# The MLP's up projection by Strassen's identity, seven half products for eight per pair of units, with token sums made once

## The reference

```python
def finish_layer(x, o_a, o_b, ga, gb, p_emb, w_oa, w_ob, w_o, g_ffn, w_up, w_down, g_ple, w_ple_gate, w_ple):
    ya = o_a.reshape(n, t, A_WIDTH).astype(x.dtype) @ w_oa
    yb = o_b.reshape(n, t, B_HEADS * B_V_DIM).astype(x.dtype) @ w_ob
    x = x + (jax.nn.sigmoid(ga) * ya + jax.nn.sigmoid(gb) * yb) @ w_o
    x = x + jnp.square(jax.nn.relu(rms_norm(x, g_ffn) @ w_up)) @ w_down
    x = x + jax.nn.sigmoid(rms_norm(x, g_ple) @ w_ple_gate) * (p_emb @ w_ple)
    return x
```

## Time and profile before

| What | Value |
|---|---|
| median of 3 runs | 1930.64 us (1929.19 to 1931.61) |
| span of the profiled execution | 1926.3 us |
| PE busy | 1867.4 us, 97% |
| PEld busy | 1731.3 us, 90% |
| DVE busy | 818.5 us, 42% |
| ACT busy | 482.1 us, 25% |
| POOL busy | 766.7 us, 40% |
| DMA | 193.40 MB, mean 100 GB/s |

### The profile page before, as it was taken

The page is one execution under the profiler, slowest core; times in us unless marked ns, Lnnn a source line. Parts: engine busy times, 40 slices in busy tenths (PEclk is TensorE's granted clock), DMA queues, the critical chain, the costliest instruction groups (busy, mean ns, idle before and its releaser), DMA issues.

```text
span 1926.3 us, 35103 instructions
## 1 busy us (share of the span) xinstructions
PE 1867.4 (97%) x13421; PEld 1731.3 (90%) x13421; DVE 818.5 (42%) x1796; ACT 482.1 (25%) x1010; POOL 766.7 (40%) x566
## 2 busy tenths in 40 slices
PE   8999999999899999999999999999999999999997
PEld 7977799998766666789999999999999999999997
DVE  5144122222848884875554421122122112355675
ACT  5232123223544443651121110010001000122222
POOL 5322123221614110105666663465446435666530
PEclk9999999999999999999999999999999999999999
DMA  7333385542011017106512421331133123211202
GB/s 237 100 130 116 109 239 183 177 161 73 1 42 55 28 47 210 56 8 211 157 51 77 162 67 44 131 137 49 44 131 131 55 87 130 88 45 44 89 22 91
DMA packets 185597, 193.40 MB, mean 100 GB/s; under 512 B 16507, under 2 KB 157659, under 8 KB 184835
## 3 DMA queue, kind: packets, MB, share of 16 engines
q1 hardware_dynamic: 168226, 161.85, 26.3%
q10 hardware_dynamic: 14816, 28.12, 4.1%
q0 software_dynamic: 2432, 1.74, 0.4%
HBM read 161.13 MB, written 63.97 MB: 117 GB/s over the span
## 4 chain that ended last, share of the span: by engine, by line
PE 51%; DVE 1%; POOL 1%; issue 1%; ACT 1%; DMA 0%; DVEq 0%; ACTq 0%; POOLq 0%
PE bank L661 17%; PE bank L662 16%; PE bank L663 16%; PE bank L2621 1%; POOL w_ple_lo L2309 0%; DVE x_res L2516 0%; PE bank L2581 0%; DMA f_gates<-gate_d 0%; POOL wu_lo_tail L2439 0%; DVE f_hg L2514 0%; ACT tail_square L2387 0%; ACT ple_sig L2380 0%; DVE f_tmp L2511 0%; PE bank L2546 0%; PE bank L2544 0%
## 5 line engine op out<-in xcount | busy, mean ns | idle before, releaser
L661 PE MATMUL bank<-h_hi,wu_hi_tail 128*128 128x352 f32 x960 | 310.4, 323 | 1.5 <-POOL wu_lo_tail L2439 1.5
L662 PE MATMUL bank<-h_lo,wu_hi_tail 128*128 128x352 f32 x960 | 307.9, 321 | 0.0
L663 PE MATMUL bank<-h_hi,wu_lo_tail 128*128 128x352 f32 x960 | 307.8, 321 | 0.0
L2437 POOL TENSOR_TENSOR wu_hi_tail<-w_stage_tail,ones 128x1024 fp32r<-128x1024 f32 x88 | 167.3, 1901 | 245.5 <-PE bank L663 162.1
L661 PE MATMUL bank<-a_hi,wu_hi_tail 128*128 128x352 f32 x768 | 247.8, 323 | 0.0
L662 PE MATMUL bank<-a_lo,wu_hi_tail 128*128 128x352 f32 x768 | 246.2, 321 | 0.0
L663 PE MATMUL bank<-a_hi,wu_lo_tail 128*128 128x352 f32 x768 | 246.0, 320 | 0.0
L2439 POOL TENSOR_TENSOR wu_lo_tail<-w_stage_tail,wu_hi_tail 128x1024 fp32r<-128x1024 f32 x88 | 219.7, 2497 | 6.9
L2390 ACT ACTIVATE a_hi<-f_hg 128x352 f32 x96 | 47.9, 499 | 597.8 <-DVE f_hg L2500 597.8
L2483 DVE TENSOR_TENSOR x_res<-bank,x_res 128x352 f32 x120 | 63.0, 525 | 301.5 <-PE bank L663 301.3
L661 PEld LDWEIGHTS bank<-h_hi,wu_hi_tail 128*128 128x128 f32 x960 | 180.1, 188 | 2.0 <-POOL wu_lo_tail L2439 1.8
(11 more groups left out here) (333 smaller groups left out, 3707.4 us busy)
## 6 DMA issues: line engine op xcount, KB each, us to landing
w_stage_tail<-in_w_up SPq DMA_DIRECT2D x32, 512.0 KB, 4.0
w_stage_tail<-in_w_down SPq DMA_DIRECT2D x32, 512.0 KB, 3.8
gate_d<-gate_out ACTq DMA_DIRECT2D x16, 528.0 KB, 3.5
f_gates<-gate_d ACTq DMA_DIRECT2D x24, 352.0 KB, 3.9
w_stage_gates<-in_w_in SPq DMA_DIRECT2D x16, 512.0 KB, 6.9
ws_ring<-in_cache_win_k SPq DMA_DIRECT2D x8, 1024.0 KB, 5.8
ws_ring<-in_cache_win_v SPq DMA_DIRECT2D x8, 1024.0 KB, 6.5
ls_keys<-in_cache_ckv SPq DMA_DIRECT2D x64, 128.0 KB, 2.2
```

Of the source, the lines that this page charges most:

```text
L661: pe.matmul(out, w, a, start=n == 0, stop=False)
L662: pe.matmul(out, w, b, start=False, stop=False)
L663: last = pe.matmul(out, v, a, start=False, stop=n == len(ks) - 1)
L2437: pool.tensor_tensor(g.wu_hi[:, j], g.w_stage[:, j], one, ALU.mult).then_inc(g.w_hi, 1)
```

## The change

Hidden units are taken in 16 pairs (`NP`). For one pair the up product is a 2 x 2 block product: rows are the two units, the inner blocks are the two halves of the 1024 features, columns the two halves of the tokens (`HALF` = 528). Strassen's identity gives its four quadrants c11, c12, c21, c22 from seven products m1 to m7 of a weight sum and a token sum, each 128 rows, four k tiles and 2 x 264 columns. The seven token sums and their high and low parts (`k_sum`, `k_hi`, `k_lo`) are made once: four under the output projection, unit by unit (`take_output_unit` on DVE, `high_of_unit` on ACT, `low_of_unit` on POOL), three in pair 0. They are of x itself: the gain g_ffn goes into the weights (`scale_quad` on POOL, in place) and the factor comes in `finish_quad`. Per pair DVE makes the five weight sums (`sum_entry`), ACT rounds each product's weights (`high_entry`), POOL makes the low part (`low_entry`); these use a ring of three slots (`wait_slot`: a slot is free when the product three entries back is done). The quadrants are gathered in SBUF: ACT copies a first product out of PSUM, DVE adds or subtracts the others (`take_back`), `finish_quad` takes the positive part and multiplies by the factor, ACT squares and rounds, DVE makes the low part (`low_quad`).

The down step follows pair by pair with K 256: entries d0 to d3 of two output units each, six matmuls per chunk, banks 4 to 7 in turn, added to x by DVE at once (`add_down`). d0 to d3 of a pair come between m3 and m6 of the next; in the last pair they come after m4, and those of the last pair itself at the end, where DVE also adds the squares (`add_last_square`), ACT rounds and squares x, and POOL makes its low part (`split_last`). The gain g_ple goes into the weights of the embedding step (`split_ple`). SP loads quarters of a pair's weights (256 KB) and quarters of the down weights in one program order (`load_mlp`), with a cache copy per pair. All engines' programs of the MLP are written out, without loops. The core of the diff ("..." where lines are left out):

```diff
+HALF = T // 2
+CW = HALF // 2
+NP = FF // (2 * P)
+Q = 4 * P
+SUMS = {"m2": 1, "m6": 2, "m1": 3, "m5": 4, "m7": 5}
+PRODUCTS = ("m2", "m3", "m6", "m1", "m5", "m7", "m4")
+DOWN = ("d0", "d1", "d2", "d3")
+TOKENS = {"m2": 0, "m3": 1, "m6": 2, "m1": 3, "m5": 4, "m7": 5, "m4": 6}
+BANKS = {"m2": 0, "m3": 2, "m6": 0, "m1": 4, "m5": 6, "m7": 0, "m4": 2}
...
+def entries_of(i):
+    if i == 0:
+        return PRODUCTS
+    if i == NP - 1:
+        return PRODUCTS + DOWN
+    return DOWN if i == NP else PRODUCTS[:2] + DOWN + PRODUCTS[2:]
...
-    Step(g, "merge", None, (g.o_hi, g.o_lo), z, per_unit=6)
-    Step(g, "residual", g.w_o[0], z, h, gain=1)
-    for f in range(NF):
-        Step(g, "up", g.w_up[0, :, f * D:(f + 1) * D], h, a)
-        out, gain = (h, 2) if f == NF - 1 else (None, None)
-        Step(g, "residual", g.w_down[0, f * D:(f + 1) * D, :], a, out, gain)
-    Step(g, "ple", g.w_ple_gate[0], h, per_unit=6)
-
-    factors = [g.steps[2], g.steps[-1]]
-    steps = g.steps
-    ups = [st for st in steps if st.kind == "up"]
-    assert len(ups) * (KD // 2) == 2 * NSEQ
+    merge = Step(g, "merge", None, (g.o_hi, g.o_lo), z, per_unit=6)
+    out = g.out_step = Step(g, "residual", g.w_o[0], z)
+    ple = Step(g, "ple", g.w_ple_gate[0], h3, per_unit=6)
 
...
+def take_output_unit(dve, g, m):
+    st = g.out_step
+    for c in range(NCH):
+        n = NCH * m + c
+        x = g.x[:, m:m + 1, c * CH:(c + 1) * CH]
+        bank = (NCH * (m % 2) + c) % 6
+        dve.wait_ge(g.full, st.chunk + n + 1)
+        dve.tensor_tensor(x, g.bank[:, bank:bank + 1, :CH], x, ALU.add).then_inc(g.free, 1)
+        if m < KD - 1 or c < NCH - 1:
+            add_square(dve, g, g.rstd_bc, c, n + 1)
+        if m == KD - 1 and c == 1:
+            sum_entry(dve, g, 0, "m2")
+    dve.wait_ge(g.free, st.chunk + NCH * (m + 1))
+    k = m % 4
+    near, far = g.x[:, k, :HALF], g.x[:, k, HALF:]
+    if m < 4:
+        dve.tensor_tensor(g.k_sum[2][:, k, :], near, far, ALU.add).then_inc(g.k_sum_s, 1)
+    else:
+        dve.tensor_tensor(g.k_sum[1][:, k, :], far, g.x[:, m, HALF:], ALU.subtract).then_inc(g.k_sum_s, 1)
+        dve.tensor_tensor(g.k_sum[3][:, k, :], near, g.x[:, m, HALF:], ALU.add).then_inc(g.k_sum_s, 1)
+    if m == KD - 1:
+        for at, n in ((15, 1), (16, 3)):
+            dve.wait_ge(g.k_hi_s, at)
+            dve.tensor_tensor(g.k_lo[n][:, 3, :], g.k_sum[n][:, 3, :], g.k_hi[n][:, 3, :].bitcast(F32), ALU.subtract).then_inc(g.k_lo_dve, 1)
+        add_square(dve, g, g.rstd_bc, NCH - 1, NCH * KD)
...
+def wait_slot(eng, g, i, name):
+    n = ENTRY[i, name]
+    if n >= 3:
+        eng.wait_ge(g.m_done, ENDS[n - 3])
+    else:
+        eng.wait_ge(g.full, g.out_step.chunk + NCH * (KD if n else KD - 1))
...
+def scale_quad(pool, g, i, name):
+    n, _ = quad_of(i, name)
+    k = 4 * (int(name[2]) - 1)
+    raw = g.raw[n][:, :].rearrange("p (k c) -> p k c", k=4)
+    wait_raw(pool, g, i, name)
+    pool.tensor_tensor(raw, raw, g.gains[:, 1, k:k + 4].unsqueeze(2).to_broadcast([P, 4, P]), ALU.mult).then_inc(g.gained, 1)
...
+def low_entry(pool, g, i, name):
+    s = slot_of(i, name)
+    src = g.e_sum[s] if name in SUMS else single_of(g, i, name)
+    pool.wait_ge(g.e_hi_s, ENTRY[i, name] + 1)
+    pool.tensor_tensor(g.e_lo[s][:, :], src[:, :], g.e_hi[s][:, :].bitcast(F32), ALU.subtract).then_inc(g.e_ready, 1)
...
+def sum_entry(dve, g, i, name):
+    one, other, op = {"m2": ("w21", "w22", ALU.add), "m6": ("w21", "w11", ALU.subtract), "m1": ("w11", "w22", ALU.add),
+                      "m5": ("w11", "w12", ALU.add), "m7": ("w12", "w22", ALU.subtract)}[name]
+    dve.wait_ge(g.gained, 4 * i + max(GAINED[one], GAINED[other]))
+    wait_slot(dve, g, i, name)
+    dve.tensor_tensor(g.e_sum[slot_of(i, name)][:, :], g.raw[quad_of(i, one)[0]][:, :], g.raw[quad_of(i, other)[0]][:, :],
+                      op).then_inc(g.e_sum_s, 1)
...
+def split_mlp(pool, g):
+    for i in range(NP):
+        if i == 0:
+            scale_quad(pool, g, 0, "w21")
+            scale_quad(pool, g, 0, "w22")
+        low_entry(pool, g, i, "m2")
+        if i == 0:
+            scale_quad(pool, g, 0, "w11")
+        low_entry(pool, g, i, "m3")
+        if 0 < i < NP - 1:
+            for name in DOWN:
+                low_entry(pool, g, i, name)
+        low_entry(pool, g, i, "m6")
+        if i == 0:
+            pool.wait_ge(g.stat_s, 2)
+            inverse_root(pool, g, g.stat[:, :], g.stat[:, :], 1.0 / D, g.mean_s, 1, g.root_s)
+        scale_quad(pool, g, i, "w12")
+        low_entry(pool, g, i, "m1")
+        low_entry(pool, g, i, "m5")
+        if i == 0:
+            pool.wait_ge(g.k_hi_s, 18)
+            pool.tensor_tensor(g.k_lo[5][:, :, :], g.k_sum[5][:, :, :], g.k_hi[5][:, :, :].bitcast(F32), ALU.subtract).then_inc(g.k_lo_pool, 1)
+        if 0 < i < NP - 1:
+            scale_quad(pool, g, i + 1, "w21")
+        low_entry(pool, g, i, "m7")
+        if i == 0:
+            scale_quad(pool, g, i + 1, "w21")
+        if i + 1 < NP:
+            scale_quad(pool, g, i + 1, "w22")
+        low_entry(pool, g, i, "m4")
+        if i + 1 < NP:
+            scale_quad(pool, g, i + 1, "w11")
+    for name in DOWN:
+        low_entry(pool, g, NP - 1, name)
+def split_last(pool, g, stage, split, at):
+    pool.wait_ge(g.w_loaded[0], (g.steps[-1].turn + 1) * 16)
+    pool.wait_ge(g.e_ready, ENTRY[NP - 1, "m4"] + 1)
+    split_ple(pool, g, stage, split, 0, at + 1)
+    for name in DOWN[:3]:
+        low_entry(pool, g, NP, name)
+    for n in range(NCH * KD):
+        if n == 6:
+            low_entry(pool, g, NP, "d3")
+        m, c = divmod(n, NCH)
+        cols = slice(c * CH, (c + 1) * CH)
+        pool.wait_ge(g.h3_hi_s, n + 1)
+        pool.tensor_tensor(g.h3[1][:, m, cols], g.x[:, m, cols], g.h3[0][:, m, cols].bitcast(F32), ALU.subtract).then_inc(g.h3_lo_s, 1)
+def split_ple(pool, g, stage, split, j, n):
+    one = g.ones[:, 0:1].unsqueeze(2).to_broadcast([P, KD, P])
+    pool.tensor_tensor(stage[:, j], stage[:, j], g.gains[:, 2, :].unsqueeze(2).to_broadcast([P, KD, P]), ALU.mult).then_inc(g.ple_gained, 1)
+    pool.wait_ge(g.ple_gained, n - g.steps[-1].unit)
+    pool.tensor_tensor(split[:, j, 0], stage[:, j], one, ALU.mult).then_inc(g.w_hi, 1)
+    pool.wait_ge(g.w_hi, n)
+    pool.tensor_tensor(split[:, j, 1], stage[:, j], split[:, j, 0].bitcast(F32), ALU.subtract).then_inc(g.w_split, 1)
+def multiply_product(pe, g, i, name):
+    s, n, bank = slot_of(i, name), TOKENS[name], BANKS[name]
+    w, v = (x[s][:, :].rearrange("p (k c) -> p k c", k=4) for x in (g.e_hi, g.e_lo))
+    pe.wait_ge(g.e_ready, ENTRY[i, name] + 1)
+    for c in range(2):
+        out, cols = g.bank[:, bank + c, :CW], slice(c * CW, (c + 1) * CW)
+        for k in range(4):
+            a, b = g.k_hi[n][:, k, cols], g.k_lo[n][:, k, cols]
+            pe.matmul(out, w[:, k], a, start=k == 0, stop=False)
+            pe.matmul(out, w[:, k], b, start=False, stop=False)
+            last = pe.matmul(out, v[:, k], a, start=False, stop=k == 3)
+    last.then_inc(g.m_done, 1)
+def multiply_down(pe, g, i, name):
+    s, e = slot_of(i, name), int(name[1])
+    w, v = (x[s][:, :].rearrange("p (k c) -> p k c", k=2) for x in (g.e_hi, g.e_lo))
+    a_hi, a_lo = g.a[1 if i == NP else 0]
+    pe.wait_ge(g.e_ready, ENTRY[i, name] + 1)
+    for q in range(6):
+        n = 6 * e + q
+        unit, c = slice(q // 3 * P, (q // 3 + 1) * P), q % 3
+        if n == 0:
+            pe.wait_ge(g.a_lo_s, 4 * i)
+            if i < NP:
+                pe.wait_ge(g.c_first, 4 * (i + 1 if i == NP - 1 else i))
+                pe.wait_ge(g.c_s, 12 * (i if i == NP - 1 else i - 1) + 7)
+        if n >= 4 or i == NP:
+            pe.wait_ge(g.x_added, 24 * (i - 1) + n - 3)
+        out, cols = g.bank[:, 4 + n % 4, :CH], slice(c * CH, (c + 1) * CH)
+        for k in range(2):
+            pe.matmul(out, w[:, k, unit], a_hi[:, k, cols], start=k == 0, stop=False)
+            pe.matmul(out, w[:, k, unit], a_lo[:, k, cols], start=False, stop=False)
+            last = pe.matmul(out, v[:, k, unit], a_hi[:, k, cols], start=False, stop=k == 1)
+        last.then_inc(g.m_done, 1)
...
+            if name == "m2":
+                if i == 0:
+                    pe.wait_ge(g.free, st.chunk + NCH * KD - 4)
+                    pe.wait_ge(g.k_lo_pool, 8)
+                else:
+                    pe.wait_ge(g.c_s, 12 * (i - 1) + 8)
+            if name == "m3":
+                if i == 0:
+                    pe.wait_ge(g.free, st.chunk + NCH * KD - 2)
+                    pe.wait_ge(g.k_lo_pool, 14)
+                    pe.wait_ge(g.k_lo_dve, 1)
+                else:
+                    pe.wait_ge(g.c_s, 12 * (i - 1) + 11)
+            if name == "m6":
+                pe.wait_ge(g.c_first, 4 * i + 2)
+            if name == "m1":
+                if i == 0:
+                    pe.wait_ge(g.free, st.chunk + NCH * KD)
+                    pe.wait_ge(g.k_lo_dve, 2)
+                    spread_products(pe, g, 0, 0, CW)
```

(100 more changed lines are left out.)

546 lines of the change are left out of this document (395 added, 151 removed).

## The result

The changed kernel takes 1943.52 us (median of four runs, 1940.81 to 1948.08) against 1929.91 for the kernel before on the same chip (1928.61 to 1931.61): a ratio of 1.0071, 95% interval 1.0055 to 1.0088. That is slower by more than 0.2%. The forecast was 1935, with a range of 1906 to 1955.

A forecast was written before the change was run, and what follows sets the result against it. TensorE, busy throughout the MLP, was taken to bound the kernel. Terms -38.2 + 15.5 + 7 + 6.2 + 8.4 + 2.6 + 3.4 = +4.9 us; 1926.3 + 4.9 + 4.3 = 1935.5, forecast 1935, range 1906 to 1955.

The forecast's parts named there:

- products of 264 columns: Up product on TensorE: 2688 matmuls of 264 columns at 122 ns replace 2304 of 352 columns; -38.2 us.
- start: First pair: ends near E+40.7 us instead of E+20.5 (E: end of output projection), waiting on POOL and DVE; +15.5 us.
- 14 pair boundaries: Between pairs: m2 0.1, m3 0.25 and d0 0.2 us late, 0.5 us each; +7 us (0 to 18).
- last pair: Last pair: m6 2.5 us late and down chunk 4 3.65 late, behind DVE's quadrants; +6.2 us (4 to 8).
- last down step: Final down step: DVE squares and POOL low parts hold each other, 1.28 us a chunk; +8.4 us.
- seam: Into the embedding step: unit 1's split takes the gain too, +2.1, and POOL meeting DVE, 0.5; +2.6 us.
- clock: TensorE's clock falls twice, after the gaps at m7 and chunk 4, 1.7 us each; +3.4 us (0 to 7).
- Rival D: Up product: 264 columns cost no less than 288, 132 ns, +27 us; 1962 us, chance 0.05.
- rival B: Start, boundaries, last down step: POOL and DVE collide more rarely; sum -16.7 us, 1914 us, chance 0.33.
- Rival E: Pair boundaries cost 1.5 us instead of 0.5, m2's chain or a quad being late; +14, 1949 us, chance 0.10.
- rival C: Last down step and last pair: clock falls to 0.50 for longer; +12.5 and 2 more, 1950 us, chance 0.11.
- Forecast A: Whole kernel: the main case with all terms as summed; 1935 us, own range 1924 to 1946, chance 0.41.

The follow-up runs named there:

- e5: Changed kernel with VectorE adding one column of each square instead of 352 in the last down step; 1934.48 us, one run.
- e1: Changed kernel with VectorE's weight sum for the next pair's m2 moved ahead of the two take-backs of m5; 1942.60 us, ratio to before 1.0062.
- e8: Changed kernel with the edit of e1, and c12's low part moved behind the last finished quadrant; 1929.10 us, ratio to before 0.9994.
- e2: Changed kernel with POOL's 2112-column low part of the fifth token group cut into four of 528 at the start; 1943.35 us.
- e9: Changed kernel with unread matmuls added in three TensorE idle stretches: ahead of first pair's m7, last pair's m6, and the gate; 1944.13 us.
- e10: Changed kernel with the fifth token group's low part moved from POOL to VectorE, into its wait for the root; 1941.04 us.
- e12: As e10, but sixth token sum ahead of the sums' copy, fifth low part behind m5's weight sum, sixth ahead of c22's take-back; 1938.10 us.
- e7: Changed kernel with e4, e8, e10, last-pair reordering, gate by rows and feature sum behind the second token group joined; 1919.01 us, ratio to before 0.9938.
- e11: e7 with the start of e12 and the token inputs' low part behind the factors' diagonal; 1914.33 us, ratio to before 0.9919.
- e4: Changed kernel with the embedding weight's low part moved from POOL (eight operations) to VectorE (one); 1939.30 us, ratio to before 1.0047.

## Why the prediction came out as it did

The sum was +4.9 us on the profiled execution; measured it is +12.8, of which the terms give 12.5:

| Term | Forecast | Measured | From |
|---|---|---|---|
| products of 264 columns | -38.2 | -39.5 | 2688 x 121.5 ns = 326.6, before 366.1 |
| down in groups of six | 0 | +1.6 | 2304 x 159.6 ns = 367.7, before 366.1 |
| start | +15.5 | +16.9 | 1045.72 to 1087.37, 41.65, less 20.4 for the products and 4.3 |
| 14 pair boundaries | +7 | +12.7 | 14 x (44.31 - 43.40) |
| last pair | +6.2 | +8.0 | 51.42 - 43.40 |
| last down step | +8.4 | +7.7 | 25.52 - 23.0, and 5.2 ahead of the gate |
| seam | +2.6 | +2.1 | unit 1 waits 3.59, before 1.47 |
| clock, and what else is left of the embedding step | +3.4 | +3.1 | first embedding unit +3.5, the rest of the embedding step +1.7, less the 2.1 |
| other | 0 | -0.1 | output projection ends 0.7 later; 0.8 of small gaps before |

**Right, with its mechanism.** The spacing at 264 columns was forecast at 122 ns and is 121.5. Rival D is out, and the products saved 39 us as their count says. The Trainium skill, "TensorE: Matmul & The Clock Gate", section "Back-to-back issue gap", has a formula that gives 112.5 ns; the page states it for a matmul by itself and not for a stream with weight loads, and the trace of this stream shows 11.5 ns over the pure columns, not 2.5. The start was walked to E+40.7 us and took 41.65, in part by luck: the pair itself ended at E+39.4, and the next m2 then waited 2.0 us for its low part, which the walk hadn't. The walk's own numbers, 40.7 - 20.5 - 4.3, give 15.9 and not 15.5. The gap ahead of m7, from start to start less one spacing, was forecast at 4.9 and is 4.0. The last pair's two gaps were forecast at 2.5 and 3.65 us and are 2.97 and 3.15 by the same count. The last down step was forecast at +8.4 and is +7.7: the squares are held behind POOL's low parts, but a chunk costs 1.18 us instead of 1.28, because the two settle into a step in which each square loses 0.3 us and each low part 0.23. e5 shows that this term is the two holding each other, and so rival B is out for this stage.

**Mis-sized.** The boundary is the step that was furthest off: I had 0.5 us for each, as m2 0.1, m3 0.25 and d0 0.2 late (0.55, and 7.7 for fourteen). Measured, m2 is 0.7 late, m3 and d0 0.1 each. I took the weight sum for m2 behind c12's chain as almost in time; the finish of c12 takes 0.86 more than alone beside POOL's scaling for the next pair, and the sum queues behind it. e1 shows that the order of this one sum doesn't decide alone: as soon as m2 is in time, m3 is late by as much. e8 shows what does: with the low quadrant moved too, 14.4 us come back, about what the change had lost against before (13.6). The term was neither a capacity nor a collision that must be paid, and that was the larger mistake: I priced an order of instructions as if it were a load. Rival E had the right place and sign, at 1.5 us a boundary where 0.9 was measured.

**The clock.** Two falls were forecast, at m7 and at the fifth chunk. In the profiled run five came. The one at m7 came and cost nothing that shows, since what follows waits for VectorE; at the fifth chunk none came in the changed kernel, but one in e2, e8, e9, e10 and e12. The two of the seam follow waits of 5.0 and 3.6 us that I had priced, but not as idle of TensorE; by the spacing of the matmuls they cost about 1.1 and 1.6 us (an estimate), and the rest of the 3.1 in the table is mostly the wait for the embedding weight's low part, 1.34 us instead of 0.45. That the forecast of 3.4 comes near is luck: the falls were other ones. In the last down step itself the clock stays at 1.00 through 25.5 us, so rival C is out for that stage; in the last pair the clock fell for 3.4 us, which the last pair's row holds. The Trainium skill, same page, section "A second HAM failure mode: psum-queue depth-cycling", was weighed there; no run here shows the clock going to and fro within the groups of six: between 1100 and 1690 us, with 24 such groups in each pair, it is at 1.00 in all of them.

**The chances.** Forecast A was the right case by its rows (the start, the held squares, a boundary of 0.9 us, nearer its 0.5 than E's 1.5). By the time alone it isn't told: 1943.5 lies nearer E's 1949 than A's 1935. A's own range of 1924 to 1946 holds the time, and slower was the likeliest of the three signs, for the reason given: small terms of order and collision, each of 2 to 17 us, add up to more than the 39 us saved. The misses mostly add and don't cancel: boundaries +5.7, last pair +1.8, the groups of six +1.6, start +1.4.

## What to carry to other kernels

Work taken off the bounding engine is worth its length only if the engines beside it still deliver in time: after such a change, read each stage's waits, find the order that makes the last operand late, and move it; 29 us came back here with the same arithmetic. When a moved operation helps its own waiter and nothing in total, look at who stood behind it in the same queue, and move that as well. A slot in which an engine is idle is not free for a long operation if the operation it waits for runs on the engine that it can hold.

## What the hardware showed that was not expected

VectorE and POOL hold each other in both directions, even where one of them has almost nothing to do: POOL's operation on nine columns took 2.31 us beside a 2112-column operation of VectorE and 0.20 without, and VectorE's weight sum 4.99 beside POOL's low part and 0.68 without. The one that started first was not slowed: VectorE's operations on 2112 columns took 2.34 to 2.36 us in all 19 places in the starts of the changed kernel, e7, e10, e11 and e12 where they began ahead of POOL's, while POOL's 512-column low part, which began 0.8 us later in 17 of them, took 2.65 or 2.66 instead of 1.29. Where POOL's began first they took 3.4. The Trainium skill, "SBUF — State Buffer", section "SBUF: two separate sides", says that the pair of ports they share is held by the one that starts first for its whole instruction; these rows agree. VectorE's additions from PSUM went on undisturbed, 0.52 us on average over all 384.

After idle of a few us TensorE's clock fell to 0.50 for 3.4 to 10.2 us, and the length differed between runs at one and the same place: in the last sums and transposes 3.4 us in the changed kernel's profile and 10.2 in that of e4. The runs of the changed kernel also lie 7.3 us apart, those of before 3.0; that the falls make this difference wasn't shown. The fastest of the four has the highest mean clock (0.990 over the span, the others 0.985 to 0.986), but two with the same 0.986 lie 5.9 us apart.
